# Input projection of a hybrid block: order of the first pair's low parts, of the rotation's loads, and of the output-gate Silu

## The reference

```
proj = x @ w_in                      # 1024 x 1024 x 4872 columns
aq, ak, av, dqkv, dbeta, da, dz, gates = split(proj)
aq, ak = apply_rope(aq), apply_rope(ak)          # the rotation
y_attn = banded_sink_attention(aq, ak, av)
dqkv   = silu(causal_depthwise_conv(dqkv, conv_w))
beta   = sigmoid(dbeta);  g = -exp(a_log) * softplus(da + dt_bias)
o_dn   = gated_delta_rule(l2(dq), l2(dk), dv, beta, g)    # chunks of 64
o_dn   = rmsnorm(o_dn) * silu(dz)                # dz: the output gate
merged = sigmoid(gateA) * (y_attn @ w_a) + sigmoid(gateB) * (o_dn @ w_d)
x = layer_norm(alpha * x + merged @ w_out)
x = layer_norm(alpha * x + relu(x @ w_up)**2 @ w_down)
```

## Time and profile before

| | |
|---|---|
| median of 3 runs | 1398.19 us (1397.06 to 1398.72) |
| profiled execution, its own time | 1397.5 us |
| its span, first to last instruction | 1395.7 us |
| PE busy | 1373.6 us, 98% |
| DVE, ACT, POOL busy | 73%, 44%, 13% |
| granted TensorE clock, mean | 0.997 |

### The profile page before, as it was taken

How to read it: one execution, slowest core, us unless ns; L and a number is a source line. 1 busy time by engine, 2 the same in 40 slices (tenths; PEclk the granted TensorE clock), 3 DMA queues, 4 the chain that set the end, 5 groups by cost and what they waited for, 6 DMA issues and landing times.

```text
span 1395.7 us, 21990 instructions
## 1 busy us (share of the span) xinstructions
PE 1373.6 (98%) x8400; PEld 1140.1 (82%) x8400; DVE 1025.1 (73%) x1890; ACT 607.8 (44%) x1306; POOL 177.7 (13%) x163
## 2 busy tenths in 40 slices
PE   9999998999999999999999999999999999999997
PEld 8788887787888888788888888888888888888885
DVE  7999885855888888655358796766665777777778
ACT  4655534432344444532113455455554544444540
POOL 4322322230000000235800000000000000000002
PEclk9999999999999999999999999999999999999999
DMA  6232344675443542244612153444335875555422
GB/s 215 91 121 106 121 162 157 223 230 172 120 108 99 133 111 56 80 151 153 231 81 110 52 190 121 166 166 166 151 126 220 302 240 176 161 165 180 128 69 120
DMA packets 123497, 206.83 MB, mean 148 GB/s; under 512 B 40865, under 2 KB 61569, under 8 KB 121089
## 3 DMA queue, kind: packets, MB, share of 16 engines
q1 hardware_dynamic: 113312, 183.93, 40.1%
q10 hardware_dynamic: 10080, 21.50, 4.1%
HBM read 142.92 MB, written 62.47 MB: 147 GB/s over the span
## 4 chain that ended last, share of the span: by engine, by line
PE 87%; DVE 6%; DMA 4%; SPq 2%; issue 1%; ACT 0%; ACTq 0%; POOL 0%; DVEq 0%; POOLq 0%
PE ps L2590 6%; PE ps L2588 6%; PE ps L2589 6%; PE ps L2209 6%; PE ps L2571 6%; PE ps L2572 6%; PE ps L2573 6%; PE ps L2157 5%; PE ps L2158 5%; PE ps L2159 5%; PE ps L2275 4%; PE ps L2096 4%; PE ps L2097 4%; PE ps L2095 4%; PE ps L2465 2%; PE ps L2469 2%
## 5 line engine op out<-in xcount | busy, mean ns | idle before, releaser
L2588 PE MATMUL ps<-thi,shi 128*128 128x512 f32 x416 | 161.8, 389 | 0.0
L2589 PE MATMUL ps<-tlow,shi 128*128 128x512 f32 x416 | 161.8, 389 | 0.0
L2590 PE MATMUL ps<-thi,slow 128*128 128x512 f32 x416 | 161.8, 389 | 0.0
L943 ACT ACTIVATE thi<-b 128x512 fp32r<-128x512 f32 x104 | 65.5, 630 | 108.0 <-PE ps L2590 108.0
L1979 DVE TENSOR_TENSOR tlow<-b,thi 128x512 fp32r<-128x512 f32 x104 | 71.8, 690 | 52.7 <-ACT thi L943 52.6
L2589 PEld LDWEIGHTS ps<-tlow,shi 128*128 128x128 f32 x416 | 78.1, 188 | 16.3
L933 POOL TENSOR_TENSOR zt<-zt,ln2gb 128x256 f32<-128x256 f32 x4 | 3.4, 852 | 690.7 <-ACT zt L1394 690.7
L2590 PEld LDWEIGHTS ps<-thi,slow 128*128 128x128 f32 x416 | 78.1, 188 | 16.2
L2588 PEld LDWEIGHTS ps<-thi,shi 128*128 128x128 f32 x416 | 78.1, 188 | 16.0
L1972 DVE TENSOR_TENSOR slow<-sraw,shi 128x512 fp32r<-128x512 f32 x104 | 71.3, 686 | 21.7 <-ACT shi L943 20.6
L943 ACT ACTIVATE shi<-sraw 128x512 fp32r<-128x512 f32 x104 | 65.1, 626 | 31.6 <-DMA zt<-xpark 16.4
(11 more groups left out here) (445 smaller groups left out, 3827.5 us busy)
## 6 DMA issues: line engine op xcount, KB each, us to landing
raw<-in_wblk SPq DMA_DIRECT2D x55, 512.0 KB, 4.5
sraw<-hpark SPq DMA_DIRECT2D x104, 256.0 KB, 2.8
hpark<-hq SPq DMA_DIRECT2D x16, 1024.0 KB, 4.9
b<-in_wblk SPq DMA_DIRECT2D x64, 256.0 KB, 3.5
wraw<-in_wblk SPq DMA_DIRECT2D x30, 512.0 KB, 4.0
hpark<-hq SPq DMA_DIRECT2D x16, 768.0 KB, 4.9
park<-cb ACTq DMA_DIRECT2D x34, 256.0 KB, 3.9
park<-cacc ACTq DMA_DIRECT2D x12, 512.0 KB, 3.2
```

What stands on the lines that cost most here:

```text
L943: cp = lambda o_, i_: act.activation(o_, i_, ACT.Copy)
L2588: mm(outp, shi[s][:, ts], thi[m][:, :], start=first, stop=False, skip_group_check=True)
L2589: mm(outp, shi[s][:, ts], tlow[m][:, :], start=False, stop=False, skip_group_check=True)
L2590: return mm(outp, slow[s][:, ts], thi[m][:, :], start=False, stop=final, skip_group_check=True)
```

## The change

1. **First pair, DVE.** The low parts of pair 0 are made in the order in which PE reads them, with A22 later and S4 ahead of T3. So that the load that overwrites `raw` 0 does not come too early, SP waits in its turn 1 for four low parts (the fourth is A22's) instead of three.
2. **Output gate, ACT.** In turns 9 and 10, `store_pair` with its Silu comes after `in_snap(n, 2)` instead of ahead of `in_hi(n+1, "S1")`.
3. **Rotation, DVE and SP.** The second half block of a turn is rotated in the next turn of DVE, after the low parts of A11, A22 and A12. SP loads it in its turn n+2, after that turn's weight loads, and stores it ahead of the load of the first one. The decay's loads move in between.

```diff
+PREP0 = ("A11", "A12", "S1", "A22", "S2", "S4", "S3")
...
 for n in range(1, N_IP + 1):
     sp.wait_ge(tx_sum, 4 * n)
-    sp.wait_ge(up_w, 7 * (n - 1) + 3)
+    sp.wait_ge(up_w, 7 * (n - 1) + (3 if n > 1 else 4))
...
-    before, (first, second) = ROPE_AT.get(n - 2, (None, None))[1], ROPE_AT.get(n - 1, (None, None))
+    before, first = ROPE_AT.get(n - 2, (None, None))[1], ROPE_AT.get(n - 1, (None, None))[0]
+    if before is not None:
+        rope_load(before)
+    if n > DEC0 + 1:
+        dec_load(2 * (n - DEC0) - 1)
     if before is not None:
         rope_store(before)
     if first is not None:
         rope_load(first)
-    if n > DEC0 + 1:
-        dec_load(2 * (n - DEC0) - 1)
+    if n > DEC0:
+        dec_load(2 * (n - DEC0))
     if first is not None:
         rope_store(first)
-    if n > DEC0:
-        dec_load(2 * (n - DEC0))
-    if second is not None:
-        rope_load(second)
...
                 in_snap(n, 1)
-                if n > N_DN // 2:
+                if n > N_DN // 2 and not B_DZ < 2 * n < B_GATE + 1:
                     store_pair(n - 1)
                 if ahead:
                     in_hi(n + 1, "S1")
...
                 in_snap(n, 2)
+                if n > N_DN // 2 and B_DZ < 2 * n < B_GATE + 1:
+                    store_pair(n - 1)
...
-            in_lo(0, "A22", "A12", "S1")
+            in_lo(0, "A12", "S1")
             t_lo(0)
-            in_lo(0, "S2")
+            in_lo(0, "A22", "S2")
             t_lo(1)
+            in_lo(0, "S4")
             t_lo(2)
-            in_lo(0, "S4", "S3")
+            in_lo(0, "S3")
             t_lo(3)
...
                 in_lo(n + 1, "A11", "A22", "A12")
...
+                if ROPE_AT.get(n - 1, (None, None))[1] is not None:
+                    rope(ROPE_AT[n - 1][1])
                 combine_in(n, 0)
...
                 in_lo(n + 1, "S3")
-                if ROPE_AT.get(n, (None, None))[1] is not None:
-                    rope(ROPE_AT[n][1])
```

More of the change, by code:

```diff
@@ L883, in in_sums @@
                 if n:
-                    pool.wait_ge(up_w, 7 * (n - 1) + PREP.index("S4") + 1)
+                    pool.wait_ge(up_w, 7 * (n - 1) + (PREP if n > 1 else PREP0).index("S4") + 1)
                 pool.tensor_tensor(s4raw, IA["A12"], own("S2"), ALU.subtract).then_inc(tx_sum, 1)
@@ L1472, in in_lo @@
                     hi, lo, src = ip_piece(n, k)
-                    assert PREP[ic["n"] % 7] == k
+                    assert (PREP if n else PREP0)[ic["n"] % 7] == k
                     ic["n"] += 1
-                    dve.wait_ge(up_hi, ic["n"])
+                    dve.wait_ge(up_hi, 7 * n + PREP.index(k) + 1)
                     if k in ("S1", "S2"):
@@ L2134, in in7 @@
                 for i, (wk, xk, b) in enumerate(IPROD):
-                    pe.wait_ge(up_w, 7 * n + PREP.index(wk) + 1)
+                    pe.wait_ge(up_w, 7 * n + (PREP if n else PREP0).index(wk) + 1)
                     if n == 0 and xk in IT_ORDER:
```

## The result

The changed kernel takes 1409.51 us (median of 4 runs, 1408.64 to 1410.56); the kernel before, run beside it, 1397.62 (4 runs, 1396.81 to 1398.72). The ratio is 1.0085 with a 95% interval of 1.0067 to 1.0102, so it is **11.9 us slower**. I had forecast 1397.8 and a range up to 1400.6.

What follows compares the result with a forecast made beforehand. PE, busy 98% of the span, was taken as the bound, its idle time priced against the rotation chain. First pair +0.4, rotation -1.2, load collisions +0.4: net -0.4, 1397.1 us profiled, 1397.8 us as median; range 1394.5 to 1400.6.

Steps and rivals of the forecast that it cites:

- First pair: Pair 0: the first wait goes, but SP's later load delays S4; +0.4 us, between 0.7 gained and 0.9 lost.
- Pair 1 absorbs at most 0.1 of it: Behind pair 0: DVE has no more slack than before, so pair 1 takes back at most 0.1 us.
- Silu: Pair 9: the wait of 1.89 us ahead of S3 and 0.12 us of restart go, -2.0 us.
- Rotation up to pair 9: Half block 0 there at 197.4, half block 1 rotated from 206.2, so pair 9 waits until 211.1: +2.6 us.
- the 2.5 us that I took from row 292.10: Extra time until a rotation load issued behind weight loads is used, applied to half block 0's load.
- the rule of the Trainium skill that I cited there: A queue's descriptors are consumed in ring order on each DMA engine; cited as speaking against moving the rotation load.
- Rotation in pairs 10 to 12: Pair 11's weights leave at 235.3, S4 of pair 12 starts at 282.5; the stage ends 1.2 us earlier.
- load 4 starts 1.7 us behind the weights, and takes 6.3 us, used at 243.3: Pairs 10 to 12: half block 4's rotation load, issued behind pair 11's weights, sets when DVE rotates it.
- My own list of what would show me wrong: Pair 9 without a wait, PE held in pairs 10 to 12 by low parts behind a rotation, or pair 11's loads before 232.
- No weights are waited for after it: Behind S4 of pair 12, PE waits for no more weights; the stage's 1.2 us gain was closed there.
- Rival (b): Slower: pair 9 waits 2.6 us, PE runs at 1.2 GHz, loads 2, 4, 6 run long; +3.0, 1401.2 us; chance 0.13.
- what I let the clock cost in my sum: Behind pair 9's wait: the sum held nothing for matmuls at half clock; 2.4 GHz was assumed from S4 of pair 10.

Runs made afterwards that it cites:

- run 3: The kernel before with the rotation part of the change alone: 1404.0 us, +6.3 over the kernel before.
- Run 9: The changed kernel with the last rotation load issued ahead of the decay load in SP's last turn alone: 1402.95 us, +4.5 over the kernel before.
- 2: The kernel before with the first pair's part alone: 1399.2 us, +1.1 over the kernel before.
- 4: The kernel before with the Silu's and the first pair's parts, without the rotation part: 1397.0 us, -0.8 against the kernel before.
- 8: The kernel before with the Silu's part and the rotation loads of half blocks 4 and 6 issued behind the weights, DVE's order unchanged: 1401.5 us.
- 10: The kernel before with Silu's part, weights of pairs 11 to 13 ahead of the waiting rotation store, half blocks 4 and 6 loaded and rotated later: 1396.6 us.
- 11: As 10, but DVE rotates half blocks 4 and 6 at the end of the turn, as in the kernel before: 1401.4 us.
- 14: The changed kernel with DVE making the decay's arguments of a turn's second tile ahead of the rotation: 1407.9 us, +10.3 over the kernel before.
- 1: The kernel before with the Silu's part alone: 1395.9 us, -1.4 against the kernel before.
- run 5: The kernel before with the Silu's and the rotation parts, without the first pair's: 1406.1 us, +8.4 over the kernel before.
- 7: The changed kernel with the decay loads behind the rotation loads and stores as before, in all turns: 1408.6 us, +10.8 over the kernel before.
- 12: The changed kernel with half block 0 loaded and rotated as in the kernel before: 1405.5 us, +6.7 over the kernel before.
- 13: As 10, with DVE making the decay's arguments of a turn's second tile ahead of the rotation: 1397.1 us, -1.5 against the kernel before.
- 15: The changed kernel with half block 0 as before and the last rotation load ahead of the decay load: 1402.3 us, +4.5 over the kernel before.
- 6: The kernel before with the first pair's and the rotation parts, without the Silu's: 1406.5 us, +8.4 over the kernel before.

## Why the prediction was wrong

**First pair: sign right, +0.4 us against 1.1 measured alone.** SP's load left at 39.95 (forecast 39.8), and S2 waited for ACT's copy as forecast (43.15, before 43.18). S4 started at 47.32 (47.0). The term that was missing is S3: it waited 0.45 us more, since POOL's first sum there took 3.82 us beside DVE's low parts and held up ACT's high part of S1 and the copy behind it. "Pair 1 absorbs at most 0.1 of it" held within a tenth: with the first pair alone, 1.6 us more at pair 1 were 1.5 at pair 9.

**Silu: the wait went, the -2.0 us didn't stay.** Alone the kernel keeps 1 to 1.4 of it, which the interval does not tell from nothing. At the start of pair 11 it was worth 4.2. Beside the moved rotation it costs 2.1.

**Rotation up to pair 9: the place right, the number helped by luck.** Half block 0 was used at 197.69 (forecast 197.4), half block 1 at 207.03 (206.2), and pair 9 started at 212.07 after 2.21 us of wait (211.1). But the load of half block 0 left at 189.41, 1.3 us later than forecast, and was used 8.3 us after that, not 9.3: the 2.5 us that I took from row 292.10 were 1.5. The rotation took 3 and not 2 us, beside POOL, and `combine_in` with `decay_sums` 1.9 and not 2.9. So the errors cancelled. That a load behind the weights is used late did show; the rule of the Trainium skill that I cited there ("DMA: Bandwidth & Descriptors", "Queues, rings and completion order") agrees.

**Rotation in pairs 10 to 12: the step that failed.** Load 2 left at 218.54 (218.3) and was used at 223.10 (223.1). Then one step after another ran longer than priced: two of the three instructions of that rotation took 1.78 and 1.67 us, so the rotation took 4.1 us and not 2.0, and from store to next load it was 2.7, not 2.0. Load 3 gave some of it back (used after 4.6 us, not 5.9), and pair 11's weights left at 236.94 (235.3). From there on the loop itself was mis-sized:

| step of the loop, us | priced | measured, from 236.94 | measured, from 260.44 |
|---|---|---|---|
| weights to next rotation load | 1.7 | 2.0 | 1.8 |
| that load to its rotation | 6.3 | 7.4 | 7.8 |
| rotation to its store | 2.0 | 3.1 | 3.1 |
| store to the next load | 2.0 | 2.6 | 2.9 |
| that load to its rotation | 6.8, then 4.8 | 5.9 | 4.0 |
| rotation, store, weights | 2.4 | 2.5 | 2.5 |
| loop | 21.2, then 19.1 | 23.5 | 22.0 |

The line "load 4 starts 1.7 us behind the weights, and takes 6.3 us, used at 243.3" is the one whose mechanism was wrong. Half block 4 was used at 246.31, and did not wait for its load at all: in DVE's order it stands behind A12's low part, and that row and the rotation's first took 1.77 us each beside POOL's sums. (In run 3, where the rotation did wait for this load, it was used 6.8 us after issue; here that would be 245.7, an estimate. So the place behind the low part costs some 0.6 us, and the slow rows the 1.1 of the next step.) My own list of what would show me wrong had DVE holding PE's low parts behind a rotation; what happened is the reverse, a rotation held behind low parts. Instead of 1.2 us gained, 6.6 were lost ahead of pair 13, the first pair's part included.

**The last turn: a term that was missing.** "No weights are waited for after it" was right, and I stopped there. The decay load that the diff moves ahead of the rotation load waits for ACT's decay store (issued at 301.94, the load leaves at 306.30), and in the last turn nothing comes after to absorb it. DVE's rotation in the changed kernel, against 299.37 in the earlier trace rows:

```profile
314.95 0.69 DVE L1559 TENSOR_TENSOR rraw<-rraw,rtab 128x512 f32<-128x512 f32 x1 [8.95 <-DMA rswp<-park]
```

Behind it stand DVE's last combinations and arguments, ACT's last stores (320.77 against 312.77) and the first loads of the next stage: 3.7 us of tail. Run 9 shows it.

**The clock.** Rival (b) came closest: slower, by the start of pair 9 and by long loads behind it, but at 1401.2 us, without the slow rotation rows and without the tail. It put the clock at some tenths. The windows of 330 to 350 us, before and after (busy us and instructions of PE, PEld, DVE, ACT, POOL; granted clock; DMA share; GB/s):

```profile
330.00:350.00 20.00, 19.97 (x309) 15.58 (x309) 12.96 (x40) 5.07 (x22) 0.00 (x0) 1.00 0.36 95
```

```profile
330.00:350.00 20.00, 16.04 (x192) 11.61 (x190) 12.21 (x35) 3.00 (x9) 0.00 (x0) 0.83 0.57 164
```

Behind the wait of 3.96 us TensorE ran a part of this stretch at 1.2 GHz. Over all 17 traces the rest goes with the clock granted in the 10 us from the `tb` matmul on: it is 1066.7 to 1066.9 where that is 1.00 (before, 2, 4, 8, 10, 11, 14), 1068.2 to 1068.4 where it is 0.83 or 0.84 (1, 3, 5, 7, 12, 13, 15), 1068.7 at 0.76 (6), and 1069.5 at 0.74 and 0.68 (changed, 9). So the 2.8 us are the clock's. What makes it fall is not the length of that wait by itself; runs 9, 8 and 3, whose `tb` matmul waited 2.29, 2.23 and 3.75 us:

```profile
336.06:346.06 10.00, 10.00 (x122) 7.41 (x123) 3.19 (x8) 2.57 (x5) 0.00 (x0) 0.68 0.34 89
333.52:343.52 10.00, 10.00 (x167) 7.28 (x169) 4.92 (x10) 2.57 (x5) 0.00 (x0) 1.00 0.47 128
332.15:342.15 10.00, 10.00 (x141) 7.01 (x142) 4.50 (x10) 2.57 (x5) 0.00 (x0) 0.83 0.44 109
```

The same holds in the projection: behind the 2.21 us ahead of pair 9 the granted clock was 1.00 from 212 to 240, behind the 2.31 us in pair 10 it was 0.72 from 244 to 250, and in run 5 it was 0.83 in the 10 us behind 1.96 us ahead of pair 9. The cause of the fall stays open. Nor is it a matter of the changed kernel alone: twenty executions of the kernel before, run beside runs 13 to 15, have mean granted clocks of 0.995 to 0.998 over the whole span, and the four of the changed kernel 0.993 or 0.994. The rule of the Trainium skill that I cited ("TensorE: Matmul & The Clock Gate", "HAM oscillation — how this bites in real kernels") is told of waits for transfers that are long enough to turn the clock down; I had left that condition out, so pair 9 speaks against my use of it, not against the page. Also wrong was what I let the clock cost in my sum, nothing.

## What to carry to other kernels

When a step is moved on one engine, write out the loop that closes through the other engines, and compare its length with the time that the bound engine has for a turn: two engines in series behind a transfer are priced by what stands ahead in each one's order, not by the transfer. Look at the last turn by itself, where a wait that other turns absorb has nothing behind it. And the effects of the parts of a change may not be added, even of parts that alone measure within 1.5 us of nothing: their delays meet in one chain, so time them together before either is kept.

## What the runs showed of the hardware

The same DVE instruction (two operands in SBUF, 128x512) takes 0.69 us alone and 1.77 beside POOL's sums, and POOL's take 1.3 alone and 1.6 beside it. In pair 0 one of POOL's took 2.87 us before, and in the changed kernel 3.82:

```profile
45.64 3.82 POOL L876 TENSOR_TENSOR ipS1r<-raw 128x512 f32<-128x512 f32 x1 [9.14 <-DMA raw<-in_wblk]
```

The Trainium skill, page "SBUF — State Buffer", section "Who interferes with whom", says that a DVE instruction with two SBUF inputs contends with a GpSimd instruction that reads SBUF; these rows agree. A DVE instruction of the same size with one operand in PSUM kept its time beside POOL, in the changed kernel:

```profile
200.72 0.68 DVE L1488 TENSOR_TENSOR cb<-cb,ps 128x512 f32<-128x512 f32 x1
...
200.78 1.29 POOL L882 TENSOR_TENSOR ipS2r<-ipS1r,raw 128x512 f32<-128x512 f32 x1 [1.26 <-PE ps L2163]
```

What I had not expected is that a wait of 2 us on a third engine, PE, decides whether the two meet.
